# RMS norms in a two-block transformer kernel: sums of squares as rows in PSUM instead of columns that are spread

## What is computed

```python
def rms_norm(x, g):
    xf = x.astype(jnp.float32)
    y = xf * lax.rsqrt(jnp.mean(xf * xf, axis=-1, keepdims=True) + NORM_EPS)
    return (y * g.astype(jnp.float32)).astype(x.dtype)

    x = x + rms_norm(mix, attn_post_norm[l])
    h = rms_norm(x, ffn_pre_norm[l])
    f = (jax.nn.silu(h @ w_gate[l]) * (h @ w_up[l])) @ w_down[l]
    x = x + rms_norm(f, ffn_post_norm[l])
```

## Time and profile before

| | us |
|---|---|
| median of 3 runs | 1918.43 |
| lowest and highest | 1917.65, 1918.82 |
| the profiled execution's own time | 1918.23 |
| its span in the trace | 1916.3 |

### The profile page before, as it was taken

How to read it: one execution, slowest core, us unless ns; L and a number is a source line. 1 busy time by engine, 2 the same in 40 slices (tenths; PEclk the granted TensorE clock), 3 DMA queues, 4 the chain that set the end, 5 groups by cost and what they waited for, 6 DMA issues and landing times.

```text
span 1916.3 us, 25712 instructions
## 1 busy us (share of the span) xinstructions
PE 1875.6 (98%) x9416; PEld 1511.1 (79%) x9416; DVE 820.6 (43%) x1396; ACT 436.3 (23%) x893; POOL 1241.5 (65%) x747
## 2 busy tenths in 40 slices
PE   8999999999999999999999999999999999999997
PEld 6886568888888898767888888889787888888886
DVE  6346864533331045253543334004994463334103
ACT  4344862211110021132311111003334331111000
POOL 7975546866676558653876667666656686666662
PEclk9999999999999999999999999999999999999999
DMA  6341002323232214211242323221323223333311
GB/s 207 122 131 45 2 1 78 98 89 99 88 120 96 91 45 154 88 46 44 78 119 89 99 88 126 96 75 56 109 67 99 77 88 97 89 99 108 106 61 44
DMA packets 44878, 168.28 MB, mean 88 GB/s; under 512 B 4984, under 2 KB 7288, under 8 KB 44672
## 3 DMA queue, kind: packets, MB, share of 16 engines
q1 hardware_dynamic: 44496, 164.56, 27.7%
q10 hardware_dynamic: 304, 2.64, 0.4%
HBM read 165.07 MB, written 2.11 MB: 87 GB/s over the span
## 4 chain that ended last, share of the span: by engine, by line
PE 87%; DVE 5%; POOL 5%; issue 2%; ACT 1%; DMA 0%; POOLq 0%; SPq 0%; DVEq 0%
PE psum L527 27%; PE psum L528 26%; PE psum L529 26%; POOL w_lo L421 2%; DVE h_lo L1413 1%; DVE tmp L1455 1%; PE psum L723 1%; DVE e_ring L1570 1%; PE psum L709 1%; POOL w_hi L418 1%; PE psum L574 1%; POOL e_ring L467 1%; PE psum L783 1%; PE psum L804 1%; PE psum L750 1%
## 5 line engine op out<-in xcount | busy, mean ns | idle before, releaser
L421 POOL TENSOR_TENSOR w_lo<-raw,w_hi 128x1024 fp32r<-128x1024 f32 (+1 forms) x286 | 749.6, 2621 | 23.8
L527 PE MATMUL psum<-h_hi,w_hi 128*128 128x512 f32 (+1 forms) x1780 | 677.4, 381 | 13.6 <-POOL w_lo L421 7.1
L529 PE MATMUL psum<-h_hi,w_lo 128*128 128x512 f32 (+1 forms) x1780 | 670.7, 377 | 0.0
L528 PE MATMUL psum<-h_lo,w_hi 128*128 128x512 f32 (+1 forms) x1780 | 670.6, 377 | 0.0
L418 POOL TENSOR_SCALAR w_hi<-raw 128x1024 fp32r<-128x1024 f32 (+1 forms) x286 | 323.0, 1129 | 484.1 <-PE psum L529 460.2
L527 PEld LDWEIGHTS psum<-h_hi,w_hi 128*128 128x128 f32 x1780 | 334.7, 188 | 88.4 <-issue 13.8
L529 PEld LDWEIGHTS psum<-h_hi,w_lo 128*128 128x128 f32 x1780 | 334.1, 188 | 68.9
L528 PEld LDWEIGHTS psum<-h_lo,w_hi 128*128 128x128 f32 x1780 | 334.3, 188 | 66.9 <-issue 0.2
L527 PE MATMUL psum<-g_hi,w_hi 128*128 128x512 f32 (+1 forms) x594 | 219.5, 369 | 0.0
L528 PE MATMUL psum<-g_lo,w_hi 128*128 128x512 f32 (+1 forms) x594 | 218.9, 369 | 0.0
L529 PE MATMUL psum<-g_hi,w_lo 128*128 128x512 f32 (+1 forms) x594 | 218.9, 369 | 0.0
(11 more groups left out here) (269 smaller groups left out, 1858.1 us busy)
## 6 DMA issues: line engine op xcount, KB each, us to landing
raw<-in_wide SPq DMA_DIRECT2D x239, 512.0 KB, 3.6
raw<-in_down SPq DMA_DIRECT2D x48, 704.0 KB, 4.1
decay<-decay_rows ACTq DMA_DIRECT2D x1, 2048.0 KB, 7.9
out<-x SPq DMA_DIRECT2D x16, 128.0 KB, 1.7
x<-in_xt SPq DMA_DIRECT2D x3, 512.0 KB, 7.0
x<-in_xt ACTq DMA_DIRECT2D x1, 512.0 KB, 4.6
o_diff<-in_angles SPq DMA_DIRECT2D x1, 512.0 KB, 10.3
cols<-in_cols SPq DMA_DIRECT2D x1, 221.0 KB, 4.4
```

Source lines behind the costliest of these rows:

```text
L421: nc.gpsimd.tensor_tensor(w_lo[:, slot, 0:w], raw[:, j % RAW, 0:w], w_hi[:, slot, 0:w].bitcast(F32), ALU.subtract).then_inc(units_split, 1)
L527: pe.matmul(out_ap, lhs[0], rhs[0], start=first, stop=False)
L528: pe.matmul(out_ap, lhs[0], rhs[1], start=False, stop=False)
L529: return pe.matmul(out_ap, lhs[1], rhs[0], start=False, stop=last)
```

## The change

At the post norms the sums are taken with the ones stationary and `total` or the squares moving, so that the product itself holds the sum of every token in every partition (`sum_rows`, `last_squares`). ACT takes the root of the 256 sums in PSUM, with the division by 1024 as scale and the epsilon as bias from a new tile `eps` (`row_roots`), and DVE the reciprocal, in place in PSUM (`half_inverse`). `half_variance`, `add_columns` and the two half spreadings are gone. At the pre norms of boundaries 1, 3, 4 and 5 the same is done for all 512 tokens: one product (`whole_row`), one root, and a reciprocal that writes `scale_row` (`inverse_row`), in place of `col_stat`, `row_stat` and `keep_row`. The pre norm of boundary 2 keeps its columns (`columns=True`), because the values of the next part are scaled by columns; so do the first norm of the kernel and the layer norm.

```diff
-            def add_columns(source, first, last, blocks=range(NB)):
-
-                for b in blocks:
-                    mm = pe.matmul(psum[:, STAT_COL, b:b + 1], source[:, b * P:(b + 1) * P], ones[:, 0:1],
-                                   start=first and b == 0, stop=last and b == NB - 1, skip_group_check=True)
-                mm.then_inc(column_added, 1)
...
+            def sum_rows(source, j, first, last):
+
+                return pe.matmul(psum[:, (STAT_ROW, STAT_COL)[j], j * H:(j + 1) * H], ones[:], source[:, j * H:(j + 1) * H], start=first, stop=last)
...
-                add_columns(squares[:, (KC - 1) % 2, :], False, blocks[-1] == NB - 1, blocks)
+                sum_rows(squares[:, (KC - 1) % 2, :], j, False, True).then_inc(row_summed, 1)
+
+            def whole_row():
+
+                n.take("squared", KC)
+                pe.wait_ge(summed, n.take("summed", KC - 1))
+                pe.matmul(psum[:, STAT_ROW, :], ones[:], total[:], start=True, stop=True).then_inc(row_summed, 1)
...
-                add_columns(total, True, False)
-                last_squares((0, 1))
+                for j in range(2):
+                    sum_rows(total, j, True, False)
+                last_squares(0)
                 for t in range(tiles):
...
-                    if t == 2:
-                        row_stat((0, 1))
...
                     if k == 0:
-                        last_squares((2, 3))
-                    if k == 2:
-                        row_stat((2, 3), STAT_COL)
+                        last_squares(1)
...
                     if t == 2:
-                        col_stat()
-                    if t == 5:
+                        if columns:
+                            col_stat()
+                        else:
+                            whole_row()
+                    if t == 5 and columns:
                         row_stat()
...
+            def row_roots(bank, place=slice(0, S)):
+
+                act.wait_ge(row_summed, n.take("row_summed"))
+                nc.scalar.activation(psum[:, bank, place], psum[:, bank, place], ACT.Sqrt, scale=1.0 / D, bias=eps[:]).then_inc(row_rooted, 1)
...
+            def inverse_row():
+
+                dve.wait_ge(row_rooted, n.take("row_rooted"))
+                v.reciprocal(scale_row[:], psum[:, STAT_ROW, :]).then_inc(row_ready, 1)
+                dve.wait_ge(row_ready, n.take("row_ready"))
...
-            def half_inverse(place):
-
-                dve.wait_ge(rooted, n.take("rooted"))
-                v.reciprocal(scale_col[:, place], root[:, place]).then_inc(col_ready, 1)
+            def half_inverse(j):
+
+                row = psum[:, (STAT_ROW, STAT_COL)[j], j * H:(j + 1) * H]
+                dve.wait_ge(row_rooted, n.take("row_rooted"))
+                v.reciprocal(row, row).then_inc(row_inverted, 1)
+                n.take("row_inverted")
...
-                half_variance(2, slice(0, 2))
                 last_out(m, 0, bias)
-                half_inverse(slice(0, 2))
-                dve.wait_ge(row_spread, n.take("row_spread"))
+                half_inverse(0)
+                dve.wait_ge(row_inverted, n.now("row_inverted"))
```

More of the change, by code:

```diff
@@ L1080, in outputs, with norm @@
                 last_square(k, 0, bias)
-                roots(slice(0, 2))
-            def norm(pre, k, bias=None):
+                row_roots(STAT_ROW, slice(0, H))
+            def norm(pre, k, bias=None, columns=False):
                 def high(j):
@@ L1265, in _ @@
             swiglu(m_ffn, 1)
-            norm("mix_pre_0", 1)
+            norm("mix_pre_0", 1, columns=True)
             act.wait_ge(forget_step, 4)
@@ L1436, in last_out, with norm @@
                     v.tensor_copy(m[:, KC - 1, place], source).then_inc(evacuated, 1)
-            def norm(m, post, pre, units, bias=None):
+            def norm(m, post, pre, units, bias=None, columns=False):
                 x_base, scaled_base, final_base = n.base.get("x_ready", 0), n.base.get("post_scaled", 0), n.base["evacuated"]
@@ L1511, in norm @@
                 n.take("post_scaled", 2 * KC)
-                if pre:
+                if columns:
                     stat()
                     keep_row()
+                elif pre:
+                    inverse_row()
             def group(u=1):
@@ L1821, in _ @@
             swiglu(m_ffn)
-            norm(m_ffn, "ffn_post", "mix_pre_0", 2)
+            norm(m_ffn, "ffn_post", "mix_pre_0", 2, columns=True)
             def forget_gates(bank):
```

64 lines of the change are left out of this document (32 added, 32 removed).

## The result

| | before | after |
|---|---|---|
| median, us | 1918.5 (6 runs, 1916.74 to 1918.82) | 1935.47 (6 runs, 1934.31 to 1936.17) |
| span of the profiled execution | 1916.3 | 1933.6 |

The ratio is 1.0088, with a 95% interval from 1.0077 to 1.0098. The kernel became 17.0 us slower. Forecast were 8.1 us, with a range that ended at 1934. The direction was right, the size was not. One of the six executions of e12_arsqrt_aligned, a variant further down, took 4685.21 us; its median leaves that slow one out, and nothing recorded says what it was.

A forecast was written before the change was run, and what follows sets the result against it. PE, busy 98%, bounds the kernel, but boundaries run through DVE and POOL: 4.4 us (boundaries 1, 3, 5), 1.3 (2), 1.1 (4) and 1.3 (6) make +8.1, so 1926.5 us, range 1919 to 1934.

The forecast's parts named there:

- the slope of the widest pair: DVE's wide reciprocals: 5.1 ns an element, from widths 8 and 16, giving 1.48 us for 256 and 2.79 for 512.
- opening, boundaries 1, 3, 5: First sums to fourth unit: POOL's run of adds, and so the fourth unit, 1.66 us later in each.
- opening, boundaries 2, 4: First sums to fourth unit: 1.28 us later in each, the first half's 0.48 being covered.
- boundary 6: DVE's chain to the end of the kernel: 1.3 us longer.
- fourth to fifth unit, four times: Pre norm's row in boundaries 1, 3, 4, 5: 7.62 us where boundary 1 had 7.81, 0.19 less.
- PE's longer pauses: Condition that would make the prediction wrong: longer waits of PE lower its granted clock; no size given.
- Step 1: First half of the post norm: `scale(0)` 0.48 us later, covered in boundaries 2, 4 and 6.
- Step 2: Second half's reciprocal between `scale(4)` and `scale(5)`: +1.33 us, less 0.1 for the variance, not regained in POOL's adds.
- Step 3: Pre norm's row, boundaries 1, 3, 4, 5: fourth to fifth unit 0.19 us less, DVE still the one waited for.
- Eight plain steps an element: Rival: wide reciprocal at 8.4 ns an element, +22.4 us, 1940.8 us; chance 0.09.
- Plain pace: Rival: wide reciprocal as fast as a plain instruction, 0.42 and 0.69 us, -6.5 us, 1912 us; chance 0.08.
- The hidden second half: Rival: second reciprocal costs nothing in boundaries 1 to 5, +1.6 us, 1920; chance 0.13, shared with slopes 2.4 to 4.2.

The follow-up runs named there:

- e12_arsqrt_aligned: Changed kernel with ACT's Abs_reciprocal_sqrt for Sqrt, no wide reciprocals (copies at the pre norms), and `eps` of 16 columns: 1876.13 us, ratio 0.9776.
- e10_shifted: Kernel before with an unused one-column tile where the changed kernel has `eps`, moving the tiles behind by 32 bytes, no instruction changed: 1922.46 us.
- e1_copies: Changed kernel with a plain copy in place of each of its 16 wide reciprocals, for timing only: 1915.34 us, ratio 0.9979.
- e5_first: Changed kernel with the first half's reciprocal made a copy, the second half's and the 512 wide ones kept: 1927.05 us, ratio 1.0047.

## Why the prediction was wrong

**The first step that failed is the reciprocal's size**, "I take the slope of the widest pair". It took 5.1 ns an element of the two slopes that the rows had (5.1 and 6.3), and it is 6.25. Nine times 0.28 and four times 0.57 us are 4.8 us. With them the sum is 8.1 + 4.8 = 12.9 us, and at equal places 13.0 to 13.4 were measured. This error alone stayed inside the forecast's own bounds (4.2 to 7 ns, 1922 to 1934 us): 1918.5 + 12.9 is 1931.4. What carried the time out of the range is the second. Term by term, in us against e10_shifted:

| | forecast | with 1.76 and 3.36 | measured |
|---|---|---|---|
| opening, boundaries 1, 3, 5 | 1.66 | 2.22 | 2.81, 1.60, 2.10 |
| opening, boundaries 2, 4 | 1.28 | 1.56 | 1.56, 1.54 |
| boundary 6 | 1.3 | 1.58 | 1.15 |
| fourth to fifth unit, four times | -0.19 | 0.38 | 0.34, 0.33, 0.35, 0.33 |

Boundary 1 has the clock's fall in it, and e10_shifted was itself 0.5 us longer than usual in boundary 3 (24.90 against 24.36 to 24.42 in the others without wide rows at the post norms; the reason isn't known); against those, boundary 3 shows 2.1. So the agreement of the sums is in part luck. With these two put right, and without any fall of the clock, the terms give 11.8 us against the 12.9, boundary 6 alone 0.43 less; the granted clock, which has no term, adds 2.3 in the profiled execution.

**The second is a part of the change that has no term at all.** The diff allocates a tile, and the forecast read it as nothing. That was worth 4.3 us by the kernel before with that tile, half of what was forecast for everything together, and no row of the trace of before points to it. The forecast put it at nothing without a reason.

**The third was named, and dismissed**: "if PE's longer pauses lower its granted clock, which no pause of the boundaries did so far". None of these had been longer than 1.02 us. At 2.02 to 2.07 us the clock fell in 7 of 18 cases, at 2.14 to 2.19 in 6 of 7. The trace of before had a warning elsewhere: behind the pause of 3.6 us, which ended at 888.70, its granted clock was 0.64 from 887 to 889 and 0.50 from 889 to 893.

**Point by point.** Step 1: the chain to `scale(0)` was right: forecast +0.48 with 1.48 us, that is +0.76 with 1.76; measured +0.74. That it is covered in boundaries 2 and 4 was wrong: the first reciprocal costs 0.69 us of its 1.34 there. Step 2: no pause in POOL's run gives it back, right, but the second costs 0.89 of 1.33, since `low(3)` runs faster beside an idle POOL. In boundaries 2 and 4 the two errors cancel (0.69 + 0.87 = 1.56), which is luck too. Step 3: right in its pieces but for the reciprocal; with it the gain of 0.19 became a loss of 0.34. That PE alone would need 6.6 us is what e1_copies shows (6.52). Of what was to be seen, PE's wait for `h_lo` was forecast at 1.8 us (2.05), for `w_lo` at 1.0 (0.93), the fifth unit's at 1.0 (1.47), and that PE's busy time would go down is true only at equal places (1875.3 against 1880.0 in e10_shifted).

**The rivals.** Eight plain steps an element: no; 6.25 ns are six times the 1.05 of a plain copy from PSUM. The repeat count of 8 in the Trainium skill, "VectorE: DVE Perf Modes", section "First, the fixed hardware budget", isn't eight such steps here, though it pointed to the right side. Plain pace: e1_copies is what that rival described; it forecast -6.5 us, and at equal places it is -7.1 (1915.34 less 1922.46), while against the kernel before it is only -3.9. The hidden second half: no, by e5_first. The change would break even, on a straight line between -7.1 us at 1.05 ns and +13.0 at 6.25, at 2.9 ns an element; the forecast said 3.3.

## What to carry to other kernels

Putting one value into every partition cost nothing for the product here (three products of 256 columns held PE no longer than the six of one column that they replaced), but each instruction behind it then works on the full width: before spreading first and inverting after, ask what the inversion costs an element, and let the engine that takes the root invert as well, if it can. Where rows give two slopes for an unseen width, keep the steeper one in the forecast or in the range, and take it from differences much larger than the scatter of short instructions. A new tile, however small, moves all tiles allocated behind it: compare a change with the kernel before at the same places, and try the places by themselves.

## What the hardware showed that was not expected

- The distance between PE's products hangs on where their tiles lie in SBUF: 0.227 to 0.233 us for 512 columns and 0.114 to 0.120 for 256, with the same instructions, and the two don't get better together. For this kernel that is 1887 to 1922 us.
- A reciprocal on DVE takes 6.25 ns an element from 32 to 512 elements a partition, from SBUF and from PSUM (1.75 us for 256). A copy of 256 takes 0.29 us from SBUF, 0.42 from PSUM. ACT's inverse root of 256 in PSUM takes 0.45 us.
- At a pause of PE of 2.0 to 2.2 us its granted clock fell to half for 3.4 us in 13 of 25 cases, and at the same pause it didn't in the others. A fall 0.03 us behind the restart cost 1.07 us in an opening, one 1.48 us behind it nothing.
- A DVE instruction with two SBUF inputs of 128x256 took 0.41 us with POOL idle and 0.85 beside an add of POOL.
